# Forgetting attention inside a two-block kernel: the bias sums made once as rows and added by products of 64 rows, and the order of VectorE around them

## What is computed

```python
log_f = jax.nn.log_sigmoid(f_f + b_forget).transpose(0, 2, 1)      # (B, H, S)

def fox_attention(q, k, v, log_f):
    cum = jnp.cumsum(log_f, axis=-1)
    ...
    s = jnp.einsum('bhqd,bhkd->bhqk', qb, k) * scale
    s = s + cb[..., :, None] - cum[..., None, :]
    s = jnp.where(kpos[None, :] <= qpos[:, None], s, NEG_INF)
    p = jax.nn.softmax(s, axis=-1)
    return jnp.einsum('bhqk,bhkd->bhqd', p, v)
```

## Time and profile before

| | us |
|---|---|
| runs, median (lowest to highest) | 1060.23 (1059.19 to 1060.81) |
| the profiled execution | 1058.21 |
| its span in the trace | 1056.3 |
| PE busy | 1017.5 |
| VectorE busy | 846.7 |
| ScalarE busy | 656.2 |
| GpSimd busy | 50.3 |

### The profile page before, as it was taken

One profiled execution on the slowest core, in us unless ns is written; L12 is line 12 of the kernel. 1 busy time (PEld: TensorE's weight loads), 2 busy tenths in 40 slices (PEclk: granted clock), 3 DMA queues, 4 the chain that ended last, 5 costly groups with the idle time before them and its releaser, 6 DMA issues.

```text
span 1056.3 us, 16489 instructions
## 1 busy us (share of the span) xinstructions
PE 1017.5 (96%) x6099; PEld 870.0 (82%) x6099; DVE 846.7 (80%) x1663; ACT 656.2 (62%) x1323; POOL 50.3 (5%) x48
## 2 busy tenths in 40 slices
PE   5989999999999999999999999999999999999997
PEld 4867888887887878887879989888887988888986
DVE  5878877768999999999979676897658876598584
ACT  6454646547888888888854676732455567763252
POOL 0201100002002010020000000000100000000010
PEclk9999999999999999999999999999999999999999
DMA  8533345342999999999955343333445434233221
GB/s 343 196 123 118 120 165 194 121 160 74 389 385 348 376 355 373 389 347 382 376 195 192 125 155 120 120 120 120 137 162 180 160 120 147 96 141 136 108 92 41
DMA packets 30177, 211.30 MB, mean 200 GB/s; under 512 B 3728, under 2 KB 3856, under 8 KB 5136
## 3 DMA queue, kind: packets, MB, share of 16 engines
q1 hardware_dynamic: 28368, 205.01, 52.2%
q10 hardware_dynamic: 1728, 5.21, 1.4%
HBM read 209.16 MB, written 1.05 MB: 199 GB/s over the span
## 4 chain that ended last, share of the span: by engine, by line
PE 71%; DVE 16%; ACT 6%; DMA 3%; issue 2%; POOL 0%; ACTq 0%; DVEq 0%; POOLq 0%; SPq 0%
PE ps L529 19%; PE ps L531 18%; PE ps L530 18%; DVE w_lo L409 7%; PE ps L1006 5%; PE ps L534 4%; DMA ring<-in_panels 2%; PE ps L689 2%; PE ps L720 1%; ACT s_buf L1973 1%; ACT w_hi L1927 1%; DVE s_buf L412 1%; DMA g_in<-in_prm 1%; PE ps L998 1%; PE ps L744 1%
## 5 line engine op out<-in xcount | busy, mean ns | idle before, releaser
L409 DVE TENSOR_TENSOR w_lo<-ring,w_hi 128x512 fp32r<-128x512 f32 x760 | 482.3, 690 | 84.9 <-ACT w_hi L1927 83.9
L1927 ACT ACTIVATE w_hi<-ring 128x512 fp32r<-128x512 f32 x760 | 423.8, 620 | 162.7 <-PE ps L531 122.0
L529 PE MATMUL ps<-w_hi,op_rows 128*128 128x512 f32 (+2 forms) x800 | 315.5, 394 | 7.6 <-DVE op_rows L409 3.1
L531 PE MATMUL ps<-w_hi,op_rows 128*128 128x512 f32 (+2 forms) x800 | 308.8, 386 | 0.0
L530 PE MATMUL ps<-w_lo,op_rows 128*128 128x512 f32 (+2 forms) x800 | 307.8, 385 | 0.0
L529 PEld LDWEIGHTS ps<-w_hi,op_rows 128*128 128x128 f32 x800 | 151.3, 189 | 40.4 <-DVE w_lo L409 5.3
L531 PEld LDWEIGHTS ps<-w_hi,op_rows 128*128 128x128 f32 x800 | 151.0, 189 | 31.0
L530 PEld LDWEIGHTS ps<-w_lo,op_rows 128*128 128x128 f32 x800 | 151.5, 189 | 27.5
L529 PE MATMUL ps<-op_rows,w_hi 128*128 128x256 f32 x544 | 157.4, 289 | 0.0
L530 PE MATMUL ps<-op_rows,w_hi 128*128 128x256 f32 x544 | 153.8, 283 | 0.0
L531 PE MATMUL ps<-op_rows,w_lo 128*128 128x256 f32 x544 | 153.7, 283 | 0.0
(11 more groups left out here) (243 smaller groups left out, 1055.1 us busy)
## 6 DMA issues: line engine op xcount, KB each, us to landing
ring<-in_panels SPq DMA_DIRECT2D x194, 1024.0 KB, 6.5
cst<-in_c ACTq DMA_DIRECT2D x1, 1229.0 KB, 7.8
buf_a<-in_pre ACTq DMA_DIRECT2D x2, 512.0 KB, 6.3
keys<-in_post ACTq DMA_DIRECT2D x2, 512.0 KB, 4.9
out<-x_tok SPq DMA_DIRECT2D x2, 512.0 KB, 2.6
cst<-in_c ACTq DMA_DIRECT2D x1, 960.0 KB, 6.5
x_tok<-in_x ACTq DMA_DIRECT2D x1, 512.0 KB, 5.0
x_tok<-in_x SPq DMA_DIRECT2D x1, 512.0 KB, 4.8
```

The lines of the kernel that those rows point to most:

```text
L409: return V.tensor_tensor(o, a, b, op)
L529: T.matmul(o, l[0], r[0], start=start, stop=False)
L531: return T.matmul(o, l[1], r[0], start=False, stop=stop)
L1927: return A.activation(o, a, ACT.Copy, scale=scale)
```

## The change

Four things change.

1. `fox_spread` on GpSimd goes. Instead GpSimd sets `fx` (256 columns) to zero at its very start, and VectorE writes, at the end of `log_in`, the 16 log gates a second time into it, spread so that of the two heads of a job the one stands in the first 64 columns of a token half and the other in the second. PE waits for this (`forget` 2 instead of 1).
2. In `fox_k` PE does two more products, of `fx` (stationary) with `ntri`, into bank 7: minus the running sums, now as rows, head 2 * job + e in partition 64 * e + job. VectorE copies bank 7 to `fsum` behind the other work of `fox_k`.
3. In `scores` the bias products take one column of `ident`, read 128 times over with step 0, as the stationary operand and `fsum` as the moving one. They have 64 rows, for each head the half in which its q·k lies, and there is one for each head and query half.
4. At take 13 VectorE calls `behind` before `feed`.

```diff
--- before.py
+++ after.py
@@ -312,7 +312,8 @@
         post = keys[:, 1024:2048]
         g_row = buf_a[:, :]
         slc_k = zin[:, TT * ZA:TT * ZA + S]
-        lfb, ntri = buf_d[:, :], c1("ntri")
+        ntri = c1("ntri")
+        fx, fsum = buf_d[:, 0:2 * P], buf_d[:, 2 * P:2 * P + S]
         cq = stat[:, 112:128].rearrange("p (a h) -> p a h", a=TT)
         ng = stat[:, 128:176].rearrange("p (a c h) -> p a c h", a=TT, c=3)
         kv2 = buf_c[:, 0:1024].rearrange("p (c g t) -> p c g t", c=2, g=2)
@@ -639,11 +640,13 @@
                 for i in range(2):
                     pair_turns(ZFK + 2 * i * P, 4 + i, z3).then_inc(side_T, 1)
                 pe.wait_ge(ld_c1, 16)
-                pe.wait_ge(forget, 1)
+                pe.wait_ge(forget, 2)
                 lf2 = stat[:, 64:80]
                 T.matmul(ps[:, 6, 0:8], ntri[:, 0:P], lf2[:, 0:8], start=True, stop=True)
                 T.matmul(ps[:, 6, 8:16], ntri[:, P:2 * P], lf2[:, 0:8], start=True, stop=False)
-                T.matmul(ps[:, 6, 8:16], ntri[:, 0:P], lf2[:, 8:16], start=False, stop=True).then_inc(side_T, 1)
+                T.matmul(ps[:, 6, 8:16], ntri[:, 0:P], lf2[:, 8:16], start=False, stop=True)
+                T.matmul(ps[:, 7, 0:S], fx[:, 0:P], ntri, start=True, stop=False)
+                T.matmul(ps[:, 7, P:S], fx[:, P:2 * P], ntri[:, 0:P], start=False, stop=True).then_inc(side_T, 1)
 
             def nsa_side(n):
                 c, kind = SIDES[n]
@@ -690,10 +693,9 @@
                     if plain:
                         continue
                     for e in range(2):
-                        l0, l1 = (lfb[:, (b * 8 + 2 * job + e) * P:(b * 8 + 2 * job + e + 1) * P] for b in range(2))
-                        m = T.matmul(ps[:, 2 + e, lo:lo + n], l0, ntri[:, 0:n], start=False, stop=a == 0)
-                        if a:
-                            m = T.matmul(ps[:, 2 + e, P:S], l1, ntri[:, 0:P], start=False, stop=True)
+                        half = slice(e * HD, (e + 1) * HD)
+                        head = ident[half, e * HD + job:e * HD + job + 1].to_broadcast([HD, P])
+                        m = T.matmul(ps[:, 2 + e, lo:lo + n], head, fsum[half, 0:n], start=False, stop=True)
                 m.then_inc(score_mm, 1)
 
             def turn(job):
@@ -1213,6 +1215,9 @@
                 dv(ts(lx, lx, 0.0, None, ALU.min))
                 settle()
                 tt(lf, lx, la, ALU.subtract).then_inc(forget, 1)
+                dve.wait_ge(po.sem, 2)
+                by_pair = [y.rearrange("p (a r e) -> p a e r", a=TT, e=2) for y in (lx, la)]
+                tt(fx.rearrange("p (a e r) -> p a e r", a=TT, e=2)[:, :, :, 0:4], *by_pair, ALU.subtract).then_inc(forget, 1)
 
             def fox_k_(_):
                 for i in range(2):
@@ -1220,6 +1225,7 @@
                     ts(fox_k[:, i * 512:(i + 1) * 512], ps[:, 4 + i, :], prmc("fk_g"), None, ALU.mult).then_inc(side, 1)
                 dve.wait_ge(side_T, 5)
                 ts(stat[:, 112:128], ps[:, 6, 0:16], -1.0, None, ALU.mult).then_inc(side, 1)
+                V.tensor_copy(fsum, ps[:, 7, 0:S]).then_inc(forget_b, 1)
 
             def lower(_):
                 lbp = prmc("lb").rearrange("p (l h) -> p l h", l=LAYERS)
@@ -1837,6 +1843,10 @@
                     cols = PIECE if n < 5 else Z5
                     dve.wait_ge(taken, t + 1)
                     V.tensor_copy(z3[:, 1, n * 512:n * 512 + cols], ps[:, 1, 0:cols]).then_inc(out_free[1], 1)
+                if t == T_Z + 13:
+                    behind(t)
+                    feed(2 * t + AHEAD)
+                    continue
                 if t != T_Z + 10:
                     feed(2 * t + AHEAD)
                 behind(t)
@@ -2337,11 +2347,6 @@
                     pool.wait_ge(head_ms, first_one + i + 1)
                     rstd_pow(stat[:, s0:s0 + TT * n]).then_inc(head_rs, 1)
 
-            def fox_spread(_):
-                pool.wait_ge(forget, 1)
-                G.tensor_copy(lfb.rearrange("p (a h q) -> p a h q", a=TT, h=8),
-                              bc(stat[:, 64:80].rearrange("p (a h) -> p a h", a=TT), P)).then_inc(forget_b, 1)
-
             def compress(step):
                 if step == 0:
                     pool.wait_ge(value_out, FOX_JOBS)
@@ -2364,7 +2369,7 @@
 
             table = {"fox_sums": lambda n: head_norms(HEADS_FOX[n:n + 1], n), "win_sums": lambda _: head_norms(HEADS_WIN, 2),
                      "slc_sums": lambda _: head_norms(HEADS_SLC, 4),
-                     "fox_k": fox_spread, "compress": compress, "head_norm": head_norm}
+                     "compress": compress, "head_norm": head_norm}
 
             def behind(t):
                 for name, arg in beside.get(t, ()):
@@ -2373,6 +2378,7 @@
 
             po(G.memset(minus_half[:, :], -0.5))
             pool.wait_ge(po.sem, po.n)
+            po(G.memset(fx, 0.0))
             norm_root(0)
             norm_root(1)
             feed(5)
```

## The result

The changed kernel took 1051.91 us (median of 4 runs, 1049.93 to 1052.49) and the kernel before 1060.52 (4 runs, 1059.19 to 1062.91) on the same chip: a ratio of 0.9911 [0.9887, 0.9935]. The profiled execution took 1052.49 where that of before took 1058.21.

What follows compares the result with a forecast made beforehand. PE, busy for 96% of the span, was taken as the bound. An earlier scores start (1.4) and three shorter jobs (4.5) summed to 5.9 us, giving 1054.3 from the median 1060.23; range 8 in 10: 1052.4 to 1056.6.

Steps and rivals of the forecast that it cites:

- Part 1: VectorE before the first scores: keys ahead of pieces, no GpSimd copy stretching them, so operands are ready at about 55.2 us.
- Part 2: PE in `fox_k`: two new full-height products cost 0.65 us, plus 0.1 for the sums' later start.
- Part 3: First scores on PE: start moves from 57.56 to 56.17 us, a gain of 1.4.
- Part 4: The four scores jobs on PE: each shrinks from 3.02 to 1.53 us, a gain of 1.49 a job.
- Part 5: How much counts: jobs 0 to 2 in full, 4.5 us; job 3 nothing, PE idling about 1.5 before `zin`'s transposes.
- A: Rival: another chain, VectorE's or ScalarE's, takes one more job's gain; gain 4.4 us, time 1055.8; chance 0.08.
- B: Rival: the bias pairs in the scores jobs don't overlap; gain 4.0 us, time 1056.2; chance 0.05.
- C: Rival: the fourth scores job (job 3) counts as well; gain 7.4 us, time 1052.8; chance 0.05.
- E: Rival: the scores jobs' step-0 stationary loads take three times as long; 4.6 us slower, 1064.8; chance 0.02.
- F: Rival: row sums arrive late, PE waits until 57.5, jobs win half; gain 1.5 to 2, 1058.5; chance 0.04.
- D: Rival: PE's new 1.5 us pause before 91 us lowers the clock, costing 1.6 us; 1055.9; chance 0.06 (upwards).

Runs made afterwards that it cites:

- e4: The changed kernel with an unread 128x1536 copy put back on GpSimd where `fox_spread` stood: 1053.09 us, ratio 0.9928 to the kernel before.
- e3: The changed kernel with VectorE's old order at take 13 (pieces ahead of the keys): 1054.46 us, ratio 0.9948 to the kernel before.
- e5: The changed kernel without the bias products in the four scores jobs: 1052.59 us, ratio 0.9935 to the kernel before.
- e6: The changed kernel with its four bias products at full height (128 rows): 1057.30 us, ratio 0.9974 to the kernel before.
- e10: The kernel before, run again with no edit: 1060.36 us, ratio 1.0003.
- e13: The changed kernel with a PE pause put back, VectorE doing five pieces ahead of the keys instead of two: 1056.41 us, ratio 0.9956 to the kernel before.
- e1: The changed kernel run again with no edit: 1054.11 us, ratio 0.9939 to the kernel before.
- e9: The changed kernel run a third time with no edit: 1052.65 us, ratio 0.9942 to the kernel before.

## Why the prediction was right or wrong

*Part 1, order and spread.* The forecast that both go and VectorE is ready before PE held: ready 1.3 us before PE (forecast 1.0). e4 and e3 correct the weights inside it: given the order, a stretched first piece costs at most 0.07, and without the order the end of GpSimd's copy wins nothing. At this place the gain is the order's.

*Part 2, the new products.* 0.65 forecast; take 14 starts 0.65 later behind the sums (0.66 to 1.31). The 0.1 for the later start of the sums was 0.08.

*Part 3, the start.* From the first sums to the first scores it was 5.62 (57.56 - 51.94) and is 4.23 (56.99 - 52.76): 1.39 won. The forecast of 1.4 had the later start of the sums in it; with that it is 1.31.

*Part 4, the jobs.* 1.51 where 1.53 was forecast. The step from q·k pairs to bias pairs held to 0.02, and e5 and e6 confirm both ends. The Trainium skill, "TensorEngine Tiling (Array Packing)", Key Properties, says that changing the tiling mode drains the engine. The runs agree in so far as a change costs time. By columns alone a job would have won 1.07 (640 columns); it won 1.51, and the 0.42 that e6 loses besides its columns fits two changes of height.

*Part 5, what counts.* Jobs 0 to 2 count in full, job 3 does not, and the wait before the `zin` transposes is 1.37 where 1.5 was forecast. Less the 0.82 by which the sums began later, the turn of job 2 is at 82.2 (forecast 82.3) and the `zin` transposes at 91.65 (forecast 91.7). What follows the transposes differs by less (958.6 and 958.2) than it does between executions of one kernel (958.2 to 960.7). From the start of the first scores to the turn of job 2 it won 4.6 (30.69 to 26.07), forecast 4.5, and from there to the `zin` transposes nothing (9.41 both times). The sum of 5.9 was measured as 5.9.

*Rivals.* A, B, C, E and F did not come. The first median, 1051.91, lies nearest to C's 1052.8, but C's mechanism is refuted: the wait of 1.37 stands where job 3's gain would have to pass, and grows to 2.0 when e5 makes the jobs shorter still. E's doubt, a stationary operand read with step 0, is answered by one row of the changed kernel (min/median/max ns): such a load takes as long as the 184 of the earlier trace rows.

```profile
L698 PEld LDWEIGHTS ps<-buf_d,ident x32: 187/188/188, 57.3 to 85.1; 64*128 64x128 f32 x32
```

D did not come, but what stood against it was weak: that the idle time before 57.56 did not bring the clock down. In that trace it did not; in another of the same kernel (e10) a fall came right behind it. The new wait of 1.37 brought no fall in the changed kernel's three traces, nor did the 2.0 in e5 or the 1.94 in e13. In the first trace of the changed kernel the clock is 1.00 at 797 to 800.5 us too, where the earlier trace rows have 0.57; the same work comes some 6 us earlier there, and the clock is 1.00 at 790 to 797 too:

```profile
797.00:800.50 3.50, 3.45 (x18) 2.57 (x17) 3.31 (x6) 1.20 (x2) 0.00 (x0) 1.00 0.45 125
```

*What failed* is the last step of the sum: "on the median of the runs shown, 1060.23, which lies 2.0 above it, **1054.3**". It took the distance between one profiled execution of before and a median of three as something that the changed kernel would have too. There the median lies 0.6 below the profiled execution (1051.91 and 1052.49), and 0.7 and 0.3 below in e1 and e9 (profiled at 1054.84 and 1052.97); in e10 the two agree (1060.36 and 1060.31). So -0.6 stands in place of +2.0, and this 2.6, less 0.2 by which the profiled execution came out above its forecast of 1052.3, is the whole miss of 2.4. That the 1052.3 came so near is part luck: besides the 5.9, the changed kernel's trace reached the transposes of the keys 0.7 later than before's and needed 0.4 less behind those of `zin`, and both are scatter.

The range fell with it, since it had no term for the scatter of a median. It rested on three runs of before, 1059.19 to 1060.81; the executions of before that were made later lie between 1055.23 and 1063.43, with the standard deviations above. By these a median of four runs moves by about 1 us by itself (1.25 x 1.7 / 2 = 1.06, an estimate), and a range of 8 in 10 needs 1.4 us to either side from this alone. Put below the lower end of 1052.4, which stood for C and the clock, that gives about 1051, and 1051.91 would have been inside. The forecast's own lower end, 1052.6, does not come out of the terms given for it either: 1059.19 - (4.6 + 1.4) is 1053.2. The two later medians, 1054.11 and 1052.65, lie in the range as it was stated. What remains, 6.9 ± 0.5 timed against 5.9 in the traces, is two errors, and no run showed a cause.

## What to carry to other kernels

Build the sum from rows of the same shape around the edited place, and check it afterwards on a stretch that starts at an event before the edit and ends at one behind it: here that stretch held to 0.02 us in three executions of the changed kernel while the whole time scattered by 1.7. Look at the granted clock of the stretch too: in one trace of before it was lower there, and the stretch 1.6 us longer. Give the range the scatter as a term of its own, take it from more than three runs, and do not carry the distance of one profiled execution from its median over to another kernel. Before counting a saved wait, ask what is late next: here one job in four won nothing, and an early table load gave back part of its gain on the next engine.

## What the runs showed of the hardware

- A GpSimd copy held up a VectorE operation with two operands in SBUF until it ended. The copy of 1.89 us before (51.86 to 53.75) made the piece that began at 51.93 end at 54.29, the one of 1.46 in e4 (52.03 to 53.49) made one that began at 52.10 end at 54.04: 0.54 and 0.55 behind the copy, for an operation that takes 0.65 to 0.69 alone. The Trainium skill, "SBUF — State Buffer", SBUF: two separate sides, calls the shared ports an exclusive lock by which the other fully blocks; these two cases agree.
- Two products of 64 rows on the two halves cost together what one of 128 rows does: 0.43 us for 256 columns, 0.22 for 128. A passage between the two heights costs about 0.2: 0.19 by the rows of before, and e6, with two more of them in a job, loses 0.42 besides its columns.
- After a pause of 1.97 us PE's granted clock was 0.61 for 4 us in one execution and 1.00 in another of the same kernel. In the first the scores job behind it took 4.63 us instead of 3.02.
